# Finished mixer inputs stored per in-projection tile, in a hybrid-mixer layer on one Trainium2 core

## What is computed

```python
mod = silu(c) @ w_ada + b_ada                      # 6 * 1024 values
h = rms_norm(x, norm1_g) * (1 + scale1) + shift1
p_lru, p_sb, p_gdn, p_rw = split(h @ w_in)
# RWKV-7, all 7 tiles of 128 channels:
pf = p_rw + (token_shift(p_rw) - p_rw) * mu
r, k, v, xw, xa, xg = split(pf)
w_log = -softplus(-(w0 + tanh(xw) @ w_up)) - 0.5
a = sigmoid(a0 + xa @ a_up);  gate = sigmoid(xg) @ g_up
# gated DeltaNet:
qkv = silu(causal_depthwise_conv([q, k, v], conv_w))   # 4 taps
o = norm(chunked_gated_delta_rule(...)) * silu(z)
mixed = sum(sigmoid(h @ w_gate[n] + b_gate[n]) * (o_n @ w_branch[n]))
x = x + gate1 * (mixed @ w_out);  h = rms_norm(x, norm2_g) * (1 + scale2) + shift2
x = x + gate2 * ((gelu(conv3(h @ w_gate)) * (h @ w_up)) @ w_down)
out = rms_norm(x, final_g)
```

## Time and profile before

| what | value |
|---|---|
| median of three runs | 2417.84 us (2416.13 to 2418.33) |
| profiled execution, its own time | 2414.55 us |
| its span in the profile | 2412.8 us |
| TensorE busy | 2160.7 us, 90% |
| DVE busy | 1147.4 us, 48% |
| ACT busy | 524.2 us, 22% |
| POOL busy | 911.7 us, 38% |
| head: first matmul of unit 0 | at 65.49 us |
| block loop | 497.73 to 1463.21 us |
| one block | about 120 us |
| last down product's end | 2386.1 us |

### The profile page before, as it was taken

How to read it: one execution, slowest core, us unless ns; L and a number is a source line. 1 busy time by engine, 2 the same in 40 slices (tenths; PEclk the granted TensorE clock), 3 DMA queues, 4 the chain that set the end, 5 groups by cost and what they waited for, 6 DMA issues and landing times.

```text
span 2412.8 us, 29277 instructions
## 1 busy us (share of the span) xinstructions
PE 2160.7 (90%) x10948; PEld 1743.6 (72%) x10948; DVE 1147.4 (48%) x1517; ACT 524.2 (22%) x790; POOL 911.7 (38%) x1106
## 2 busy tenths in 40 slices
PE   2898999988989898989898986897999999999994
PEld 1686777667777777777777775685888888888883
DVE  6644443465656565656565655525323232322324
ACT  2214432241313131313131312104101010110102
POOL 6573323311313131313131312553646565555650
PEclk7899999889999999999999998898999999999997
DMA  7561111120102020102010106410111111111111
GB/s 267 160 200 57 70 53 57 40 62 21 62 25 66 20 67 20 61 25 65 21 59 27 48 17 230 166 51 27 44 53 43 52 43 52 43 52 49 47 43 70
DMA packets 67130, 159.11 MB, mean 66 GB/s; under 512 B 7825, under 2 KB 27665, under 8 KB 66961
## 3 DMA queue, kind: packets, MB, share of 16 engines
q1 hardware_dynamic: 58160, 142.30, 17.6%
q10 hardware_dynamic: 8928, 16.26, 1.8%
HBM read 131.77 MB, written 26.76 MB: 66 GB/s over the span
## 4 chain that ended last, share of the span: by engine, by line
PE 71%; DVE 12%; ACT 6%; issue 5%; DMA 2%; POOL 2%; SPq 1%; DVEq 0%; ACTq 0%; POOLq 0%
PE gbank L463 42%; PE mbank L893 10%; PE mbank L630 8%; PE mbank L533 2%; PE gbank L553 2%; POOL w_lo L410 1%; DVE fa L1566 1%; DVE fa L1232 1%; POOL w_hi L406 1%; DVE fa L1494 1%; DMA fa<-in_w_ada 1%; DVE fa L1492 1%; PE mbank L760 1%; PE mbank L663 1%; PE mbank L542 1%
## 5 line engine op out<-in xcount | busy, mean ns | idle before, releaser
L406 POOL TENSOR_TENSOR w_hi<-w_raw,zero 128x256 fp32r<-128x256 f32 (+1 forms) x544 | 398.2, 762 | 1433.9 <-PE gbank L463 1252.2
L463 PE MATMUL gbank<-h_hi,w_hi 128*128 128x512 f32 x1760 | 720.3, 409 | 74.1 <-DVE h_lo L1252 39.7
L463 PE MATMUL gbank<-h_hi,w_lo 128*128 128x512 f32 x1760 | 707.2, 402 | 0.0
L463 PE MATMUL gbank<-h_lo,w_hi 128*128 128x512 f32 x1760 | 706.4, 401 | 0.0
L410 POOL TENSOR_TENSOR w_lo<-w_raw,w_hi 128x256 fp32r<-128x256 f32 (+1 forms) x544 | 485.6, 922 | 10.7
L463 PEld LDWEIGHTS gbank<-h_hi,w_hi 128*128 128x128 f32 x1760 | 339.4, 193 | 170.4 <-issue 63.6
L463 PEld LDWEIGHTS gbank<-h_hi,w_lo 128*128 128x128 f32 x1760 | 340.0, 193 | 75.6 <-issue 4.8
L463 PEld LDWEIGHTS gbank<-h_lo,w_hi 128*128 128x128 f32 x1760 | 340.6, 194 | 71.4 <-issue 6.1
L630 PE MATMUL mbank<-fa 128*128 128x128 f32 x1792 | 226.4, 277 | 35.7 <-DVE fa L1566 22.0
L630 PEld LDWEIGHTS mbank<-fa 128*128 128x128 f32 x1792 | 214.8, 191 | 57.3 <-DVE fa L1566 34.5
L893 PE MATMUL mbank<-ra,w_hi 128*128 128x512 f32 x704 | 218.3, 391 | 7.8 <-DVE fa L1693 4.2
(11 more groups left out here) (293 smaller groups left out, 2281.0 us busy)
## 6 DMA issues: line engine op xcount, KB each, us to landing
w_raw<-in_w_tail SPq DMA_DIRECT2D x74, 512.0 KB, 3.3
fa<-in_w_ada SPq DMA_DIRECT2D x48, 512.0 KB, 4.4
w_raw<-in_w_in SPq DMA_DIRECT2D x26, 512.0 KB, 3.3
w_raw<-in_w_mix SPq DMA_DIRECT2D x16, 640.0 KB, 4.2
fa<-in_xT SPq DMA_DIRECT2D x16, 512.0 KB, 7.9
w_raw<-in_w_gate SPq DMA_DIRECT2D x16, 512.0 KB, 3.9
sig_scr<-fa ACTq DMA_DIRECT2D x32, 256.0 KB, 2.1
fa<-sig_scr SPq DMA_DIRECT2D x16, 512.0 KB, 3.9
```

What stands on the lines that cost most here:

```text
L406: last = pool.tensor_tensor(hi[:, c], raw[:, c], zero[:, 0:1].to_broadcast([P, w]), ALU.add)
L463: mm = pe.matmul(gb[bank], w, r, start=(q == 0), stop=(q == 3 * ks - 1))
```

## The change

It has four places. The order on the engines is by hand, so the diff says what moves.

**A. Head.** The "ones" mask is loaded alone and first, the first two weight tiles stand right behind x0 and x1, the first 16 product tiles use eight buffers. The multiplication by the root moves from POOL to DVE, ACT makes both `h_hi` and the f32 h, POOL splits a whole tile of units 0 and 1 with one operation each, and TensorE does units 0 and 1 together, k by k in four banks. The remaining product tiles: 3 behind the h parts, 6 in each of three rounds, and 11 before unit 10's weights.

**B. LRU and stick-breaking stage.** The columns of `w_in` are put so that unit 10 is the LoRA input. DVE finishes each in-projection tile when it has been copied out: `shift_mix` for seven tiles, `gdn_conv` for six, `gdn_silu` for eight, with sigmoids on ACT. TensorE does the LoRA products over all tokens as 12 matmuls in steps 0 to 3. ACT stores 20 finished whole tiles.

**C. Block loop.** A block loads 16 finished tiles and, behind the output of the block before, 4 more (gate and z), without halo. Token shift, LoRA, convolution, SiLU and their sigmoids leave the block. The products `gd_g1` and `gd_g2` move to its start, and the `FILL` numbers change.

**D. Tail.** The last down product and the final norm go by halves of 512 tokens. Its k = 0 matmuls stand before the wait for the last tile's low part. POOL sums the squares. The output leaves as 16 DMAs of 256 KB.

```diff
-RW_T, GDN_T = 7, 8
-P_TILES = RW_T + GDN_T
-HALO = 3
-BLK = P + HALO
+P_TILES, P_EARLY = 20, 16
-FILL = [48, 72, 80, 96, 130, 138, 166, 174, 186, 200, 210]
-FILL_L, FILL_Y, FILL_Z = 120, 2, 1
+FILL = [10, 36, 44, 62, 94, 108, 166, 176, 188, 200, 210]
+FILL_L, FILL_Y, FILL_Z = 84, 6, 2
...
@@ SP, head
-            for t in range(18):
-                if t >= 3:
-                    sp.wait_ge(sem("ada_used"), t - 2)
-                sp.dma_start(fa[:, 12 + t % 3, :], a["w_ada"][t]).then_inc(sem(f"ada_in{t % 3}"), 16)
+            for t in range(16):
+                if t >= 8:
+                    sp.wait_ge(sem("ada_used"), t - 7)
+                sp.dma_start(fa[:, 12 + t % 8, :], a["w_ada"][t]).then_inc(sem(f"ada1_in{t % 8}"), 16)
...
@@ POOL, head
-            pool.wait_ge(sem("rstd1"), 1)
-            for k in range(KT):
-                pool.tensor_tensor(fa[:, k, :], fa[:, k, :], fa[:, 9, :], ALU.mult).then_inc(sem("h_norm"), 1)
...
@@ PE, head
+            for k in range(KT):
+                pe.wait_ge(sem("h_done"), k + 1)
+                for s in range(2):
+                    for hf in range(2):
+                        for w, r in ((0, h_hi), (0, h_lo), (1, h_hi)):
...
@@ ACT, head
             for k in range(KT):
-                act.wait_ge(sem("h_f32"), k + 1)
-                act.activation(h_hi[:, k, :], fa[:, k, :], ACT.Copy).then_inc(sem("h_hi"), 1)
+                act.wait_ge(sem("h_norm"), k + 1)
+                act.activation(h_hi[:, k, :], fa[:, k, :], ACT.Identity, bias=mod[:, k:k + 1],
+                               scale=a1[:, k:k + 1]).then_inc(sem("h_hi"), 1)
...
+                act.activation(fa[:, 12 + k % 4, :], fa[:, k, :], ACT.Identity, bias=mod[:, k:k + 1],
+                               scale=a1[:, k:k + 1]).then_inc(sem("h_f32"), 1)
...
@@ PE, stick-breaking stage
+            def lora_half(n):
+                t, hf = divmod(n, 2)
...
+                    pe.wait_ge(sem("lora_read"), n)
+                pe.matmul(gb[3], lora[:, t, :], fa[:, LT, hf * HALF:(hf + 1) * HALF], start=True,
+                          stop=True).then_inc(sem("lora_full"), 1)
...
                     sb_scores(n)
+                if n < 4:
+                    lora_half(3 * n)
                 if j < 32:
                     in_job(j, 0, 12)
                 if n >= 1:
                     sb_turn(n - 1)
+                if n < 4:
+                    lora_half(3 * n + 1)
...
@@ DVE, stick-breaking stage
+                dve.tensor_scalar(f_, e_, omu[:, t:t + 1], None, ALU.mult).then_inc(sem("mix_cur"), 1)
+                dve.wait_ge(sem("mix_cur"), u - 9)
+                dve.scalar_tensor_tensor(f_[:, 1:], e_[:, 0:S - 1], pc("rw_mu", t), f_[:, 1:], ALU.mult,
+                                         ALU.add).then_inc(sem("p_mixed"), 1)
...
@@ PE, block
                 gates(FILL[0])
-                pe.wait_ge(sem("rw_lt"), at("rw_lt", i, 3))
-                pe.wait_ge(sem("rw_o"), at("rw_o", i, 0))
-                for t in range(6):
-                    last = pe.matmul(mb[t // 4][:, (t % 4) * P:(t % 4 + 1) * P], lora[:, t, :], rw["lt"], start=True,
-                                     stop=True)
-                last.then_inc(done("rw_p1"), 1)
                 pe.wait_ge(sem("rw_sq"), at("rw_sq", i))
+                pe.wait_ge(sem("rw_o"), at("rw_o", i, 0))
                 pe.matmul(mb[2][:, 0:256], m_("bd"), rw["t1"], start=True, stop=True).then_inc(done("rw_p2"), 1)
+                pe.wait_ge(sem("gd_sq"), at("gd_sq", i))
+                pe.matmul(mb[1][:], m_("bd"), gd["sq"], start=True, stop=True).then_inc(done("gd_g1"), 1)
...
@@ ACT, block
-                act.preload_act_table_set("natural_log_exp_and_others")
                 act.wait_ge(sem("rw_p2"), at("rw_p2", i))
                 act.activation(rw["rn"], mb[2][:, 0:256], ACT.Ln, bias=eps[:, 0:1]).then_inc(done("rw_ln"), 1)
...
@@ POOL, tail
+            for n in range(2 * (KT - 1)):
+                hf, m = n // (KT - 1), n % (KT - 1) + 1
...
+                pool.tensor_tensor(acc, acc, fin_sq_slot(n), ALU.add).then_inc(sem("fin_acc"), 1)
...
@@ PE, tail
+            pe.wait_ge(sem("act_lo"), FT - 1)
+            for m in range(6):
...
+                fin_down(m, 0, 0)
+            pe.wait_ge(sem("act_lo"), FT)
+            for m in range(6):
+                fin_down(m, 0, 1).then_inc(sem("fin_full"), 1)
```

More of the change, by code:

```diff
@@ L686, in _ @@
                 gates(FILL_L)
[L687 to L688 removed]
+                gates(FILL[4])
                 pe.wait_ge(sem("gd_gbc"), at("gd_gbc", i, 2))
[L690 to L694 removed]
                 pe.wait_ge(sem("rw_x"), at("rw_x", i))
@@ L1222, in _, with fin_root @@
             ffn_hi(FT - 1, 1, 1)
-            for m in range(KT):
-                square(m, m % 2, 1, "down_read", KT * NG + m + 1)
-            root(2, gbank[:, 0:2, :].rearrange("p b s -> p (b s)"))
+            act.preload_act_table_set("natural_log_exp_and_others")
+            def fin_root(hf, bank):
+                half = fa[:, RSTD, hf * HALF:(hf + 1) * HALF]
+                act.wait_ge(sem("sq_summed"), hf + 2)
+                act.activation(half, bank, ACT.Ln, bias=eps[:, 0:1], scale=1.0 / D).then_inc(sem("ln2"), 1)
+                act.wait_ge(sem("ln2"), hf + 2)
+                act.activation(half, half, ACT.Exp, scale=-0.5).then_inc(sem("rstd"), 1)
+            for hf in range(2):
+                for m in range(KT):
+                    act.wait_ge(sem("fin_add"), hf * KT + m + 1)
+                    n = hf * (KT - 1) + m - 1
+                    if m and n >= 4:
+                        act.wait_ge(sem("fin_acc"), n - 3)
+                    act.activation(fin_sq_slot(n) if m else fa[:, ACC, hf * HALF:(hf + 1) * HALF],
+                                   fa[:, m, hf * HALF:(hf + 1) * HALF], ACT.Square).then_inc(sem("fin_sq"), 1)
+                    if hf == 1 and m == 2:
+                        fin_root(0, fin_bank[KT - 1])
+            fin_root(1, fin_bank[0])
         @block.vector
@@ L1359, in _ @@
             past, npast = m_("past"), m_("npast")
+            shift_mix(12)
             for n in range(len(SB_STEPS)):
                 sb_weights(n)
+                for u in range(13, 25):
+                    if n == max(0, 2 * u - 26) and u in RW_TILES:
+                        shift_mix(u)
+                    if n == 2 * u - 26 and u in GDN_TILES and u < 23:
+                        gdn_conv(u)
+                    if n == 2 * u - 26 + (1 if u < 23 else 0) and u in GDN_TILES:
+                        gdn_silu(u)
                 if n % 4 == 1 and n > 4:
```

518 lines of the change are left out of this document (317 added, 201 removed).

## The result

| | before | after |
|---|---|---|
| median | 2416.99 us (2416.09 to 2418.33, 4 runs) | 2401.42 us (2399.16 to 2404.68, 4 runs) |
| ratio | | 0.9936, 95% interval 0.9919 to 0.9953 |
| profiled execution, own time and span | 2414.55, 2412.8 | 2404.68, 2402.9 |
| granted clock over the span | 0.95 | 0.944 |

The change is 15.6 us faster (0.64%). I had forecast 41 us, 2377, and 2347 to 2405: the sign and the range held, the size was wrong by more than a factor of two.

A forecast was written before the change was run, and what follows sets the result against it. The prediction took TensorE, busy for 90% of the span, as the bound, so edits pay only where it stands still. Head -26.7, middle stage +15.5, block loop -10.5 and tail -19 sum to -40.7: median 2377 us, range 2347 to 2405.

The forecast's parts named there:

- Head, -28.2 forecast: Units 0 to 9: transfers bound the products, units 0 and 1 end at 68.9 instead of 97.25, -28.2 us.
- Late weights, 1.5 forecast: Unit 10's weights, queued on SP behind 11 product tiles, come late by 1.5 us (nothing to 6).
- LRU and LoRA, 15.5 forecast: LRU and stick-breaking stage: added LoRA matmuls, ACT passes and bank waits cost +15.5 us (+10 to +25); DVE's work costs nothing.
- Block loop, -10.5 forecast: Eight blocks: -4.3 us for block 0's lighter cold start and -0.9 for each of the seven others.
- about as much work at half clock: Block loop: half-clock work stays about equal, with some 4 us of it behind the wait for gd's squares.
- Tail, -19.3 forecast: Last down product and final norm by halves, sum of squares on POOL: end at 2393.5, -19.3 us.
- the change fills the 3.54 us with k = 0 products: Tail: k = 0 matmuls fill TensorE's 3.54 us wait for the last FFN tile's low part; 96 matmuls end about 2379.
- The block loop that gives nothing back: Rival, block starts: two new waits cost, later waits stay at 12.7 us; +6 a block, end 2436; chance 0.05.
- The rival in which the block starts wait less: Rival, block starts: gd's squares come before TensorE needs them; -3 to -4 us a block, 2350; chance 0.18.
- slow head transfers: Rival, head: transfers stay at 220 GB/s, 2388; chance 0.10.
- load cost twice its row: Rival, block loop: each table switch holds the next operation up by 1.28 us again; 20 us, 2398; chance 0.03.
- late in the middle stage: Rival, stick-breaking stage: POOL's splits lengthen DVE's operations, convolution steps late by 3 to 4 us; +20, 2397; chance 0.10.

The follow-up runs named there:

- The idle matmuls: Changed kernel with ten matmuls that nobody reads added between p2 and g1 in a block: 2384.20 us against 2401.4.
- the moved ones: Changed kernel with sixteen gate matmuls moved from behind g2 to between p2 and g1: 2348.93 us against 2401.4.
- w10_early: Changed kernel with unit 10's weights loaded behind six of the last eleven product tiles, not all: 2395.20 us against 2401.4.
- tail_wait: Changed kernel with the wait for the last weight tile moved behind the four output tiles that don't use it: 2393.39 us against 2401.4.

## Why the prediction was right and wrong

Of the 41 us forecast, 31 are missing in the profiled execution: about 12 in the block loop, 9 in the tail, 5 in the late weights, 4 in w_out and FFN and 2 in the head; the rest cancels.

**Head, -28.2 forecast for units 0 to 9.** They end 26.5 us earlier: right in its mechanism, 1.7 short. Transfers ran at the deep-queue rate (408 GB/s from 22 to 38 us), products at 1.23. But it was not transfer that bounded the products, as I had written: from 20.77 they follow one another on DVE, with one wait of 0.39 us for a tile, and the last ends at 41.4 where the forecast had them done by 38.7.

**Late weights, 1.5 forecast.** Mis-sized: it is about 6 us, 3.17 of waiting and half clock behind it. The run with the earlier load is 6 us faster and moves the landmark by 7.5. I had bounded the term by 6 and taken the low value without working the time out.

**LRU and LoRA, 15.5 forecast.** The LRU part lost 8.3 with the late weights in it, so about 2 without; forecast 3.2. The four steps lost 13.1 against 12.3. DVE's 41 us more in the stage cost nothing (the other 28 steps: -0.3), as said.

**Block loop, -10.5 forecast, +1.4 measured.** This step failed. Its open time came out: 13.9 us a block forecast, 94.2 / 7 = 13.5 measured, against 12.9 before, with 6.1 a block in the two new waits where I had 5.9. What failed is "about as much work at half clock". The whole loop, before and after, from the landmarks of the table:

```profile
497.73:1477.98 980.25, 862.18 (x5346) 718.31 (x5346) 573.98 (x930) 245.39 (x437) 217.49 (x256) 0.96 0.13 44
```
```profile
492.35:1474.01 981.66, 861.74 (x5250) 712.61 (x5250) 460.18 (x834) 249.54 (x381) 192.22 (x256) 0.93 0.14 46
```

96 records of LoRA left (10.6 us at 1.33 a block), yet TensorE's busy time fell by 0.4: so 10.2 us went to the clock, of the 11.9 that the loop missed. Half clock held much longer at a block's start than the 4 us that I gave it (13.6 us in the block shown, 3.4 before). And there was a stretch some 100 us into every one of the eight blocks, in the state part, of 3.4 and 6.8 us by turns, where I saw no reason for one; before, four of the eight blocks had one of 3.4. The stretches that the kernel before had 25 to 49 us into a block, ten of 3.4 us, left with the waits there. The idle matmuls (17 us) and the moved ones (19 of 47 us) show that the start's part was the clock. Why it falls in the state part, and why for 6.8 us in every second block, was not found.

By the first gate matmul behind a block's gate sigmoid, block 0 gave 2.5 of the 4.3 us forecast, and the other seven lost 3.9 where I had them gain 6.3. Block 0 has a wait of 3.73 before g1 too, and half clock behind it (501.3 to 504.7), which my -4.3 does not name. The sign that I had set for this step, a period outside 116 to 122, could not show the failure: both kernels lie inside.

I had also written that the removed DVE work would give back what the start costs. In open time it did, just: the later waits, the levels' with their new filler among them, fell by about as much as the two new ones took (47 and 49 us in the loop). The run of the kernel before with one tap suggests why the removal of 13 us is worth so little by itself: there, part of each wait that left came back at a later hand-over. A kernel with finished tiles and the old order of a block was not run, so what the order alone cost is read from the waits.

**w_out and FFN, 0 forecast, +4.0 measured.** 2.9 of it at the FFN's start. TensorE did the same work from its first matmul to the same DVE row at 1674.48, in both traces, from 1643.66 and from 1646.57:

```profile
1646.57:1674.48 27.91, 23.95 (x76) 16.12 (x77) 17.84 (x15) 17.50 (x17) 5.89 (x6) 0.73 0.00 1
```
```profile
1643.66:1674.48 30.82, 26.86 (x76) 18.19 (x77) 17.84 (x16) 17.51 (x17) 5.90 (x6) 0.65 0.00 1
```

The count of matmuls is the same 76 and 26.86 of 30.82 us are busy instead of 23.95 of 27.91: the full clock came at 1665 instead of 1661.5. Three microseconds gained were lost by that. It is not a cost of the change. From the first matmul of the branch stage to POOL's split of the last weight tile, the work is the same in all fifteen traces, and it takes between 876.0 us (before) and 879.9 (after); the run w10_early, with the whole change in it, takes 876.1, and tail_wait 878.1. So before and after happened to be the two ends.

**Tail, -19.3 forecast, -9.9 measured.** The step that failed is "the change fills the 3.54 us with k = 0 products". The wait for the last split stands ahead of them, and POOL ends it at 2360. In the kernel before, only the second half of the outputs had met that split. I costed the new order of matmuls and not the wait that the diff put in front. With the wait moved, the tail has the forecast length to 0.1 us, and its last addition ends where I had put it (28.8 us behind the split, forecast 28.6).

**Sums of mine that do not come out.** The balance of -0.3 a block is -0.6 by its own terms (13.9 - 13.2 - 1.33). The first h part at 45.1 is 44.9 by the four operations named, and the tail's -19.3 went into the sum as -19. None of these changes the outcome.

**The rivals.** The block loop that gives nothing back came true in its place, but not by its mechanism and price: the later waits did shrink, and the loop lost 1.4, not 48. The rival in which the block starts wait less did not come true, nor did slow head transfers. No load cost twice its row. DVE was not late in the middle stage. The table's landmarks add up to -9.9 in the profiled execution; the profiled execution of after lies 3.3 us above its median and that of before 2.4 below, which makes the other 5.7.

## What to carry to other kernels

When work leaves an engine that does not limit, look at once at what the limiting engine's list does with it. Here the change gave 16 us as it stood and 106 with 24 of a block's 216 filler matmuls moved into two waits, one wait moved back and one load issued earlier (the fourth edit, the table set loaded once, added nothing beside them). Where an order puts short waits of TensorE behind one another, count the half clock behind them as a cost of its own, and put filler there first. In a reordered program, read what each moved wait waits for, also where it was harmless in its old place.
